# Query products and two gated embeddings of a streaming encoder step, read as pairs of column groups

## The chip, the cores and the metric

The kernel runs on one core of one Trainium2 chip. The metric is the time of one execution on the device, in microseconds (us). Before the change it is 3810.11 us, the median of 3 runs (3791.88 to 3811.25).

## What is computed

One step of a one-layer streaming encoder, in fp32, on 512 prompt frames and 64 running frames of width 2048. The reference, cut to what matters:

```python
a = rmsnorm(x);  z = a @ w_in                       # 2048 x 7168, and 8 gate columns
mix = concat(retention(z), mlstm(z)) @ w_out        # 2048 x 2048, chunk by chunk, with states
h = x + mix
c = rmsnorm(h);  q = c @ w_peer_q                   # 2048 x 2048: 8 heads of 256
s1, s2 = q[..., :128] @ keys1.T, q[..., 128:] @ keys2.T
# top 16 of s1 and of s2, top 16 of their sums: 128 experts of 16384 for each frame
h = h + sum_k softmax(score)_k * gelu(c . peer_u[idx_k]) * peer_v[idx_k]
e = rmsnorm(h)
h = h + sigmoid(e @ w_ple_gate) * (p @ w_ple_proj)  # 2048 x 2048 and 256 x 2048
y = rmsnorm(h)
```

## The kernel before, in words

**Tiles.** Frames are handled in five blocks of 128 (`NB`): four of the prompt, and one (`SB`) that holds the 64 running frames twice. The dense part of the layer is done in three chains, `GROUPS = [[0], [1, 2], [3, SB]]`. A chain is the product with `w_in` in 14 column groups of 512 columns, with retention and mLSTM beside it on all engines, the product with `w_out` in 4 groups, and the query product with `w_peer_q` in 4 groups, in which every group also gives the scores of two heads (`pe_scores`, line 1047). Embeddings (`EMBEDS = [[0], [1, 2, 3], [SB]]`) come later, 4 groups each (`pe_embed`, line 1143).

**Weights.** All products read their weights through one buffer `W` of four slots (q = 0 to 3), 1 MB each. SyncE issues one transfer for each slot (`load_w`, line 601) as soon as TensorE has done with the slot's last content: the semaphore `used[q]`, or `mm` for a slot whose last use ends a group. Without pairing a transfer holds 4 k-tiles of 128 rows by 512 columns, and runs in pieces of 2048 bytes (line 618); four transfers make one column group. With `paired(what, g)` (line 83) a transfer holds 2 k-tiles by 1024 columns, in pieces of 4096 bytes (line 614), and eight transfers make two column groups, which both end at the eighth (`pe_pairs`, line 819). Before the change the `in` and `out` products of chains 1 and 2 are paired; chain 0, all query products and all embeddings are not.

**Experts.** Each frame's experts are gathered by rows: gather number u brings, for the 128 frames of a block, one row of 8 KB of `peer_u` each (1 MB in all, `ring`), and VectorE takes its product with the frame (line 2135). GpSimd issues these gathers (line 766), on a queue of its own. For blocks 0, 3 and `SB` a row of `peer_v` is gathered as well, 12 rows later, and VectorE adds it to `h` (line 2147). Blocks 1 and 2 get their `peer_v` part densely: a matrix of weights is built from one-hot products (`dve_build`, `act_build`, `pe_build`: line 1109), kept in DRAM and multiplied with all of `peer_v` (`pe_dense`, line 1139; 32 steps of 4 MB through `W` and a second buffer). The ring has 8 slots of 1 MB: 4 for u and 4 for v rows up to row 128, 6 for u rows from 128 to 383, then 3 and 3. There are 576 u rows and 320 v rows.

**Order.** Every engine but TensorE follows one list, merged before the launch from generators by their positions (`braid`). The position's unit is one u row: `yield x` puts what follows at row x. `CHAIN_AT`, `EMBED_AT`, `FIRST_PICK`, `LATE_PICKS`, `BUILD_AT` and `DENSE_AT` say at which rows a piece of a chain stands, and `in_at`, `out_at`, `q_at`, `pick_at`, `group_at` turn them into positions. An engine takes its list in order, so VectorE can wait at a piece of a chain while rows lie ready in the ring. For chain 1 `q_at(1, x)` is row 102.6 + 4.7x, for chain 2 `q_at(2, x)` is row 310.6 + 8.2x. The first choice of experts of a chain (`dve_picks`, line 1932 on, at `pick_at`) stands at `q_at(g, 1.5)`: rows 109.7 and 322.9, spread over 4 and 10 rows. The build of block 1's matrix waits at row 350 for the end of chain 2's query product (line 2027). The products of embedding e with the sigmoid are taken by VectorE at `group_at(e, i, ...)` (lines 2078 and 2082): for e = 0 rows 139.4, 142.9, 146.5 and 150.0 (i = 0 to 3), for e = 1 rows 544.7, 551.9, 559.2 and 566.4, at each of these three blocks one after the other, 0.3 row apart.

**TensorE.** Its order is written out: chain 0, chain 1, embedding 0, chain 2, build, dense part, embedding 1, embedding 2. In `pe_product` a piece of `p @ w_ple_proj` (`beside`, line 1186, its matmuls in line 1194) follows the products of its block; there is one bank for it in each half of PSUM, so for the second and third block it waits until VectorE has taken the block before (`e_mul`). `room` (line 1180) waits until the sigmoids of the group that used the banks last are done. Embedding 2 starts when all v rows are in (`v_used`, before line 1163). `pe_h_turn` (line 1018) transposes quarters of `h` for the query product, through banks 2 and 6 in turns.

## Time and profile before

| | |
|---|---|
| median of 3 runs | 3810.11 us (3791.88 to 3811.25) |
| the profiled execution | 3817.56 us |
| its span | 3815.7 us |
| TensorE, VectorE, ScalarE, GpSimd busy | 83%, 72%, 18%, 35% of the span |
| mean TensorE clock granted | 0.899 |
| moved by DMA | 1470.90 MB, 385 GB/s over the span |

Durations and start times in the profile are microseconds from the start of the span. A row of a timeline names start, duration, engine, line, operation, operands and, in brackets, the idle time before it and what ended it. A row of a table by stretches gives for each stretch busy time of the engines with instruction counts, then the granted clock of TensorE (1.00 is the higher of its two levels), the DMA engines' busy share and what they moved in GB/s. Queue q0 is that of GpSimd's gathers, q1 that of SyncE's transfers.

### The profile page before, as it was taken

What the parts mean: (1) busy time and instruction counts of PE and PEld (TensorE: products, weight loads), DVE (VectorE), ACT (ScalarE), POOL (GpSimd) and SP (SyncE); (2) the same over time, 40 slices, a digit from 0 to 9 for tenths busy, and PEclk for the clock granted to TensorE, in tenths of its full rate; (3) what the DMA queues carried; (4) which work ended last, traced back from release to release, by engine and by line L of the source; (5) the groups of instructions that cost most, each with busy time, mean ns of one, the idle gap of its engine ahead of it and who ended that gap; (6) DMA issues with size and microseconds to landing.
All of it is one profiled execution on the core that took longest, in us unless ns stands there. A gap on an engine that the chain in (4) does not pass through costs nothing.

```text
span 3815.7 us, 27395 instructions
## 1 busy us (share of the span) xinstructions
PE 3148.9 (83%) x9486; PEld 1696.0 (44%) x9486; DVE 2762.2 (72%) x3853; ACT 679.6 (18%) x1648; POOL 1329.1 (35%) x905
## 2 busy tenths in 40 slices
PE   8998697998885559999888645699999999888927
PEld 4447343544464234454437635344444444343403
DVE  1005987677677778878757788878788999787772
ACT  2212110222020221123202457000000000011003
POOL 0001533224235444423333522433333333246460
PEclk9999798999997769999998756899999999998968
DMA  7889999999999999999899999999999999999995
GB/s 268 283 274 342 418 417 418 417 418 419 416 398 414 390 362 417 417 417 397 328 402 408 377 365 337 357 420 420 420 420 420 420 419 412 411 417 397 413 370 185
DMA packets 333059, 1470.90 MB, mean 385 GB/s; under 512 B 28152, under 2 KB 66488, under 8 KB 198712
## 3 DMA queue, kind: packets, MB, share of 16 engines
q0 software_dynamic: 129744, 944.82, 60.6%
q1 hardware_dynamic: 192528, 512.40, 35.3%
q10 hardware_dynamic: 10648, 11.92, 1.0%
q8 instruction: 75, 1.23, 0.1%
q14 instruction: 64, 0.52, 0.0%
HBM read 1443.36 MB, written 25.69 MB: 385 GB/s over the span
## 4 chain that ended last, share of the span: by engine, by line
DMA 41%; PE 24%; DVE 9%; issue 5%; POOL 5%; ACT 3%; SPq 0%; DVEq 0%; ACTq 0%; POOLq 0%
DMA ring<-in_peer_v,eidx 21%; PE psum L830 13%; DMA ring<-in_peer_u,eidx 9%; POOL ring L766 5%; DMA W<-in_w_peer_q 5%; PE psum L808 4%; DVE ring L2135 3%; DVE arena L2147 3%; PE psum L1076 2%; PE psum L1139 2%; DMA a_scratch<-arena 1%; DMA W<-in_w_out 1%; DMA W<-in_w_ple_gate 1%; PE psum L1109 1%; PE psum L1194 1%
## 5 line engine op out<-in xcount | busy, mean ns | idle before, releaser
L766 POOL DMA_INDIRECT ring<-in_peer_u,eidx x576 | 879.6, 1527 | 1739.4 <-DVE dots L2135 1310.1
L2135 DVE CUSTOM_DVE_ANT_0 ring<-ring,cx 128x2048 f32<-128x2048 f32 x576 | 1312.1, 2285 | 207.5 <-DMA ring<-in_peer_u,eidx 205.5
L2147 DVE SCALAR_TENSOR_TENSOR arena<-ring,wts,arena 128x2048 f32<-128x2048 f32 x320 | 751.8, 2349 | 210.7 <-DMA ring<-in_peer_v,eidx 194.4
L830 PE MATMUL psum<-W,actT 128*128 128x512 f32 x1792 | 785.9, 597 | 14.0 <-DVE arena L1891 10.6
L766 POOL DMA_INDIRECT ring<-in_peer_v,eidx x320 | 446.3, 1395 | 632.6 <-DVE arena L2147 595.1
L830 PEld LDWEIGHTS psum<-W,actT 128*128 128x128 f32 x1792 | 339.7, 192 | 428.2 <-issue 417.2
L1139 PE MATMUL psum<-arena 128*128 128x512 f32 x1024 | 455.2, 605 | 22.1 <-DVE arena L2058 22.1
L808 PE MATMUL psum<-W,actT 128*128 128x512 f32 x960 | 432.3, 607 | 40.1 <-issue 28.0
L1139 PE MATMUL psum<-W,arena 128*128 128x512 f32 x1024 | 447.2, 596 | 8.7 <-DVE arena L2058 8.7
L1076 PE MATMUL psum<-actT,W 128*128 128x128 f32 (+2 forms) x1536 | 289.9, 354 | 82.8 <-DMA W<-in_w_peer_q 71.4
L1139 PEld LDWEIGHTS psum<-arena 128*128 128x128 f32 x1024 | 197.6, 195 | 269.6 <-issue 239.4
L1076 PEld LDWEIGHTS psum<-actT,W 128*128 128x128 f32 x1536 | 265.1, 210 | 106.6 <-DMA W<-in_w_peer_q 77.0
L808 PEld LDWEIGHTS psum<-W,actT 128*128 128x128 f32 x960 | 185.8, 195 | 272.7 <-issue 256.5
L1139 PEld LDWEIGHTS psum<-W,arena 128*128 128x128 f32 x1024 | 193.8, 191 | 251.1 <-issue 235.7
L830 PE MATMUL psum<-W,arena 128*128 128x512 f32 x512 | 228.5, 608 | 22.5 <-DMA W<-in_w_out 22.2
L1628 ACT ACTIVATE gel<-dots 128x8 f32<-128x8 f32 x72 | 15.1, 209 | 1098.4 <-DVE dots L2135 1098.3
L2058 DVE TENSOR_TENSOR arena<-psum,arena 128x1024 f32<-128x1024 f32 x128 | 155.8, 1218 | 29.3 <-PE psum L1139 29.3
L830 PEld LDWEIGHTS psum<-W,arena 128*128 128x128 f32 x512 | 99.3, 196 | 147.6 <-issue 121.0
L1550 ACT COPY arena<-psum 128x1024 f32<-128x1024 f32 x32 | 32.3, 1009 | 486.5 <-PE psum L1123 486.5
L808 PE MATMUL psum<-W,arena 128*128 128x512 f32 x256 | 113.7, 594 | 0.3 <-ACT arena L1431 0.3
L1109 PE MATMUL psum<-W 128*128 128x128 f32 x256 | 61.9, 422 | 44.3 <-ACT W L1525 24.2
L781 ACT ACTIVATE actT<-psum,gT 128x128 f32<-128x128 f32 x224 | 60.4, 409 | 182.6 <-PE psum L773 108.1
(283 smaller groups left out, 2149.1 us busy)
## 6 DMA issues: line engine op xcount, KB each, us to landing
W<-in_w_in SPq DMA_DIRECT2D x168, 1024.0 KB, 12.8
W<-in_peer_v SPq DMA_DIRECT2D x64, 1024.0 KB, 14.9
arena<-in_peer_v SPq DMA_DIRECT2D x64, 1024.0 KB, 17.6
W<-in_w_out SPq DMA_DIRECT2D x48, 1024.0 KB, 13.0
W<-in_w_peer_q SPq DMA_DIRECT2D x48, 1024.0 KB, 23.0
W<-in_w_ple_gate SPq DMA_DIRECT2D x48, 1024.0 KB, 16.3
actT<-a_scratch SPq DMA_DIRECT2D x64, 256.0 KB, 26.7
ring<-in_peer_u,eidx POOLq DMA_INDIRECT x576, 16.3
```

The source lines that it names most:

```text
L766: pool.indirect_dma_start(ring[:, slot, :], None, a["peer_u" if what == "u" else "peer_v"][0], off(ix, 0)).then_inc(ring_in[slot], 16)
L781: ins = act.activation(aT(k, j), bank(src_bank)[:, x * P:(x + 1) * P], ACT.Identity, scale=gT[:, gain, k:k + 1])
L808: ins = pe.matmul(bank(4 * s + j), lhs(k, j), W[:, k, :], start=(k == 0), stop=(k == KT - 1))
L830: ins = pe.matmul(bank(4 * s + j), lhs(at_k, j), w_pair(q)[:, k, s * CG:(s + 1) * CG], start=(at_k == 0), stop=(at_k == KT - 1))
L1076: ins = pe.matmul(bank(2 * (i % 2) + c // 2)[:, at:at + fresh], W[:, k, c * P:(c + 1) * P], actT[:, k, 0:fresh], start=(k == 0 and c % 2 = ...
L1109: ins = pe.matmul(bank(b % 4)[:, x * P:(x + 1) * P], hot1(b)[:, x, :], hot2(b)[:, x, :], start=True, stop=True)
L1139: ins = pe.matmul(bank(at % 3 * 2 + half), a_turned(m)[:, i // 2, x, :], v_tiles(m)[:, x, c0:c0 + 512], start=(x == 0), stop=(x == VT - 1))
L1194: ins = pe.matmul(bank(4 * (i % 2) + 3), pT(e)[:, k, at:at + P], wp[:, k, i * CG:(i + 1) * CG], start=(k == 0), stop=(k == PK - 1))
L1550: act.copy(a_turned(m).rearrange("p b x t -> p b (x t)"), psum[:, 6:8, :]).then_inc(at_c, 1)
L2058: dve.tensor_tensor(hc, psum[:, at % 3 * 2:at % 3 * 2 + 2, :], hc, ALU.add).then_inc(d_add, 1)
L2135: dve.tensor_tensor_reduce(row, row, cx[:, :], 1.0, 0.0, ALU.mult, ALU.add, dots[:, n % DEEP, c:c + 1]).then_inc(u_used, 1)
L2147: dve.scalar_tensor_tensor(out=hslot(t), in0=ring[:, slot, :], scalar=wts[:, n % DEEP, c:c + 1], in1=hslot(t), op0=ALU.mult, op1=ALU.add). ...
```

## The change

`paired` becomes true for the query products of chains 1 and 2 and for embeddings 0 and 1. `pe_pairs` takes over the pieces beside the products of an embedding: `beside(i, 0)` before the last step, all others of both groups after it. `pe_scores` gets a form for pairs: products of both groups in banks 0 to 3, the scores of the first group before the next pair's first step, those of the second after it. Quarter 2 of `h` is turned through bank 6 and quarter 3 through bank 4. ScalarE takes both groups' queries and then both groups' scores. The first choice of experts moves from `q_at(g, 1.5)` to `q_at(g, 2.6)`: rows 114.8 and 331.9. `group_at` moves to rows 142.9, 143.9, 150.0 and 151.0 for embedding 0, and to rows 551.9, 554.9, 566.4 and 569.4 for embedding 1.

```diff
 def paired(what, g):
 
-    return g > 0 and what in ("in", "out")
+    return g < 2 if what == "ple" else g > 0
...
     if i == j == 0:
-        return q_at(g, 1.5) + FIRST_PICK[g] * x
+        return q_at(g, 2.6) + FIRST_PICK[g] * x
...
 def group_at(e, i, x):
 
-    return embed_at(e, 4 + 2.2 * len(EMBEDS[e]) * (i + 1)) + x
+    n = len(EMBEDS[e])
+    if paired("ple", e):
+        return embed_at(e, 4 + 2.2 * n * (2 * (i // 2) + 2)) + n * (i % 2) + x
+    return embed_at(e, 4 + 2.2 * n * (i + 1)) + x
...
         def pe_pairs(pe, what, g, n, lhs, room, at, side, beside=None):
             for i in range(0, ZG if what == "in" else DG, 2):
                 for step in range(2 * WQ):
                     U, q = prod.use0[what, g] + i + step // WQ, step % WQ
                     pe.wait_ge(landed[q], 16 * (U + 1))
                     for s in range(2):
+                        if beside and step == 2 * WQ - 1 and s == 0:
+                            beside(i, 0)
                         for j in range(n):
...
+                    if beside and step == 2 * WQ - 1:
+                        for s in range(2):
+                            for j in range(0 if s else 1, n):
+                                beside(i + s, j)
...
+        def h_bank(g, q):
+
+            return (2, 6, 6, 4)[q] if g else (2, 6)[q % 2]
+
...
+            if paired("q", g):
+                for i in range(0, DG, 2):
+                    for step in range(2 * WQ):
+                        U, q = prod.use0["q", g] + i + step // WQ, step % WQ
+                        pe.wait_ge(landed[q], 16 * (U + 1))
+                        if i == 0 and step % 2 == 0:
+                            pe.wait_ge(n_cp, counts.quarter0["ffn", g] + (step // 2 + 1) * n)
+                        if i == step == 0:
+                            pe.wait_ge(added, DG * b0 + 3 * n)
+                        if i and step == 0:
+                            score(i - 2)
+                        for s in range(2):
+                            for c in range(4):
+                                if i and step == 0 and c % 2 == 0:
+                                    pe.wait_ge(q_taken, HH * g + 4 * (i - 2 + s) + c + 2)
+                                for k in range(2):
+                                    at_k, at = 2 * step + k, c % 2 * MAXB * P
+                                    ins = pe.matmul(bank(2 * s + c // 2)[:, at:at + fresh],
+                                                    w_pair(q)[:, k, s * CG + c * P:s * CG + (c + 1) * P], actT[:, at_k, 0:fresh],
+                                                    start=(at_k == 0 and c % 2 == 0), stop=(at_k == KT - 1 and c % 2 == 1))
+                                if step == 2 * WQ - 1:
+                                    ins.then_inc(mm, 1)
+                        if step < 2 * WQ - 1:
+                            ins.then_inc(used[q], 1)
+                        if i == 0 and step < 2:
+                            pe_h_turn(pe, g, DG - 2 + step)
+                        if i and step == 0:
+                            score(i - 1)
+                score(DG - 2)
+                score(DG - 1)
+                return
...
-                for i in range(DG):
+                def take_q(i):
                     done = HH * g + 4 * i
-                    yield q_at(g, i + 1)
+                    yield q_at(g, done_at(g, i))
...
+                together = 2 if g else 1
+                for i in range(0, DG, together):
+                    for x in range(together):
+                        yield from take_q(i + x)
+                    for x in range(together):
+                        yield from take_scores(i + x)
```

## Rows read from the trace of the kernel before

**Rows 1.** The page: span, and GB/s in 40 equal slices of it.
```profile
span 3815.7 us, 27395 instructions
GB/s 268 283 274 342 418 417 418 417 418 419 416 398 414 390 362 417 417 417 397 328 402 408 377 365 337 357 420 420 420 420 420 420 419 412 411 417 397 413 370 185
```

**Rows 2.** DMA view, 622 to 640 us: queue, packets, MB, share (pieces of 4 KB against rows).
```profile
q0 software_dynamic: 670, 4.90, 65.5%
q1 hardware_dynamic: 667, 2.60, 36.1%
```

**Rows 3.** DMA view, 2104 to 2140 us (pieces of 2 KB against rows).
```profile
q0 software_dynamic: 1652, 12.00, 80.7%
q1 hardware_dynamic: 1460, 2.89, 21.3%
```

**Rows 4.** DMA view, 650 to 840 us (4 KB), then 3600 to 3680 us (2 KB).
```profile
q1 hardware_dynamic: 5712, 22.02, 28.9%
...
q1 hardware_dynamic: 2661, 5.26, 17.5%
```

**Rows 5.** Busy time by stretches of 20 us (columns as told above).
```profile
1120.00:1140.00 20.00, 17.75 (x74) 14.84 (x73) 15.91 (x17) 3.18 (x8) 8.78 (x5) 0.83 0.91 350
1320.00:1340.00 20.00, 19.26 (x41) 8.46 (x42) 8.02 (x8) 3.46 (x4) 5.59 (x3) 0.91 0.78 283
2140.00:2160.00 20.00, 12.79 (x71) 12.09 (x70) 8.96 (x13) 5.45 (x23) 6.05 (x3) 0.90 0.74 307
2160.00:2180.00 20.00, 12.46 (x55) 11.31 (x56) 20.00 (x40) 19.37 (x47) 6.32 (x7) 0.61 0.95 353
```

**Rows 6.** VectorE's timeline: waits for query products and for embedding 0.
```profile
1093.13 0.29 DVE L1922 MAX8 arena<-arena 128x8 f32<-128x128 f32 x1 [6.78 <-ACT arena L1495]
1328.61 0.69 DVE L2078 TENSOR_TENSOR arena<-psum,arena 128x512 f32<-128x512 f32 x1 [21.31 <-ACT arena L1591]
1344.07 0.69 DVE L2078 TENSOR_TENSOR arena<-psum,arena 128x512 f32<-128x512 f32 x1 [7.40 <-ACT arena L1591]
1360.16 0.69 DVE L2078 TENSOR_TENSOR arena<-psum,arena 128x512 f32<-128x512 f32 x1 [2.61 <-ACT arena L1591]
2154.67 0.23 DVE L2027 TENSOR_SCALAR W<-eidx 128x128 uint32<-128x128 uint32 x1 [10.83 <-PE psum L1076]
```

**Rows 7.** TensorE's timeline: four of 16 query steps that waited for weights.
```profile
1071.10 8.86 PE L1076 MATMUL psum<-actT,W 128*128 128x256 f32 x32 [3.25 <-DMA W<-in_w_peer_q]
1118.73 8.86 PE L1076 MATMUL psum<-actT,W 128*128 128x256 f32 x32 [3.46 <-DMA W<-in_w_peer_q]
2135.78 7.76 PE L1076 MATMUL psum<-actT,W 128*128 128x192 f32 x32 [6.25 <-DMA W<-in_w_peer_q]
2147.69 6.94 PE L1076 MATMUL psum<-actT,W 128*128 128x192 f32 x32 [4.15 <-DMA W<-in_w_peer_q]
```

**Rows 8.** VectorE's timeline: two u rows in a row with a v row between.
```profile
1178.07 2.29 DVE L2135 CUSTOM_DVE_ANT_0 ring<-ring,cx 128x2048 f32<-128x2048 f32 x1 [0.87 <-DMA ring<-in_peer_u,eidx]
1184.49 2.29 DVE L2135 CUSTOM_DVE_ANT_0 ring<-ring,cx 128x2048 f32<-128x2048 f32 x1 [0.89 <-DMA ring<-in_peer_u,eidx]
```

**Rows 9.** TensorE's timeline: embedding 1, then the start of embedding 2.
```profile
3445.75 9.80 PE L808 MATMUL psum<-W,actT 128*128 128x512 f32 x16 [17.77 <-issue]
3458.83 7.03 PE L808 MATMUL psum<-W,actT 128*128 128x512 f32 x16
3469.13 7.03 PE L808 MATMUL psum<-W,actT 128*128 128x512 f32 x16
3642.92 1.88 PE L1194 MATMUL psum<-arena,ring 128*128 128x512 f32 x4
3728.78 6.51 PE L1163 MATMUL psum<-arena,misc 128*128 128x512 f32 x8 [83.98 <-DVE arena L2147]
```

**Rows 10.** VectorE's timeline: embedding 1 at rows 551.9, 566.4, 567.0; a late v row.
```profile
3543.00 0.69 DVE L2078 TENSOR_TENSOR arena<-psum,arena 128x512 f32<-128x512 f32 x1
3636.93 0.69 DVE L2078 TENSOR_TENSOR arena<-psum,arena 128x512 f32<-128x512 f32 x1
3645.66 0.69 DVE L2078 TENSOR_TENSOR arena<-psum,arena 128x512 f32<-128x512 f32 x1 [2.28 <-ACT arena L1591]
3695.33 2.35 DVE L2147 SCALAR_TENSOR_TENSOR arena<-ring,wts,arena 128x2048 f32<-128x2048 f32 x1 [2.56 <-DMA ring<-in_peer_v,eidx]
```

More of the change, by code:

```diff
@@ L795, in pe_product @@
             if paired(what, g):
-                pe_pairs(pe, what, g, n, lhs, room, at, side)
+                pe_pairs(pe, what, g, n, lhs, room, at, side, beside)
                 return side
@@ L817, in pe_product, with pe_pairs @@
             return side
-        def pe_pairs(pe, what, g, n, lhs, room, at, side):
+        def pe_pairs(pe, what, g, n, lhs, room, at, side, beside=None):
             for i in range(0, ZG if what == "in" else DG, 2):
@@ L1021, in pe_h_turn @@
                 pe.wait_ge(added, DG * b0 + q * n + j + 1)
-                if q >= 2:
-                    pe.wait_ge(n_cp, counts.quarter0["ffn", g] + (q - 2) * n + j + 1)
-                pe_turn(pe, "ffn", g, q, j, n, hslot(t), (2, 6)[q % 2] + j)
+                if q >= 2 and not (g and q == 3):
+                    pe.wait_ge(n_cp, counts.quarter0["ffn", g] + (q - (1 if g else 2)) * n + j + 1)
+                pe_turn(pe, "ffn", g, q, j, n, hslot(t), h_bank(g, q) + j)
         def pe_out(pe, g):
@@ L1081, in pe_scores @@
                         ins.then_inc(used[q], 1)
-                    if i == 0 and q == 0 and g:
-                        pe_h_turn(pe, g, DG - 2)
                     if i == 0 and q == 1:
@@ L1455, in turned @@
                 for j in range(n):
[L1456 removed]
+                    act_turned(act, "ffn", g, q, j, n, 1, h_bank(g, q) + j)
             def exps():
@@ L1486, in scores, with take_scores @@
                         act.copy(qT[:, c, 0:fresh], src).then_inc(q_taken, 1)
-                    yield q_at(g, i + 1.4)
+                def take_scores(i):
+                    done = HH * g + 4 * i
+                    yield q_at(g, done_at(g, i) + (0.3 if g else 0.4))
                     if i == 0:
```

4 lines of the change are left out of this document (2 added, 2 removed).

## The prediction

> **What bounds the kernel now.** I read the bytes by slices first [rows 1]. From 400 us to nearly the end they stand near 417 GB/s, a level that no slice passes by more than 3: for most of the span the DMA engines are full, and the time is the bytes divided by that level, plus the stretches where they are not full. So a change here gains in two ways only: cheaper bytes, or fewer stretches with idle DMA. The stretches that this change touches are in the table of 20 us [rows 5]: 350 GB/s at 1120 us (query product of chain 1), 283 at 1320 (embedding 0), 307 and 353 at 2140 (end of chain 2's query product). Against 418 GB/s that is 68, 135, 111 and 65 GB/s missing for 20 us each: 3.3, 6.5, 5.3 and 3.1 us of lost transfer time.
>
> VectorE's timeline says why [rows 6]. Its list is fixed, so when it waits at a piece of a chain, rows pile up in the ring, the ring fills, and then the gathers stop. It waited 6.78 us for chain 1's first scores, 31.3 us in all at embedding 0 (21.31, 7.40, 2.61), and 10.83 us at row 350 for the last step of chain 2's query product. All of these wait for TensorE, and TensorE waits for weights: 16 query steps did so [rows 7]. Those steps come 11.9 us apart (2135.78 to 2147.69), where one needs 7 to 9 us.
>
> Why the weights are slow is the step on which I rest most. SyncE's and GpSimd's queues compete. With pieces of 2 KB, 1460 of them went beside 1652 pieces of the row queue (8 KB rows and some small ones) in 36 us [rows 3]: nearly one for one, so weights got 2.89 MB against 12.00, or 80 GB/s, 13.1 us for a transfer of 1.049 MB. With pieces of 4 KB it was 667 beside 670 in 18 us [rows 2], again one for one, but 2.60 MB against 4.90: 144 GB/s, 7.3 us a transfer. The change makes query and embedding pieces 4 KB, so against a full ring their transfers should come in 7.3 us, not 13.1, and rows should be slower while they do.
>
> **The change part by part.**
>
> *Cheaper bytes.* 16 transfers each for two query products and two embeddings, 64 in all. Time per byte while a piece is in an engine: 22.02 MB in 28.9% of 190 us is 401 GB/s for 4 KB, 5.26 MB in 17.5% of 80 us is 376 for 2 KB [rows 4]. A transfer costs 2.61 instead of 2.79 us of all engines, 0.18 us less. Over 64 that is 11.5 us at most, none if DMA isn't the limit. Embedding 1's 16 fall where I expect another limit (below), so I take 48: -8.6 us; ends -11.5 and 0. The Trainium skill, Perfetto Trace Analysis, section DMA Optimizations, says that going from 2 KB to 4 KB or 8 KB can improve throughput dramatically. By the rows it is 7%, and only on these bytes; the page gives no figure, so the sum goes by the rows.
>
> *Chain 1's query product.* Both groups now end at the eighth transfer, which before was TensorE's step at 1118.73 [rows 7], 48 us after the fourth at 1071.10. The choice of experts stands 5.2 rows later in VectorE's list. A row, u and v, takes 6.42 us when DMA is full [rows 8]: 33 us. With the old transfers VectorE would wait 15 us longer. At 7.3 us a transfer the four steps more are 29 us, and the transfer before them comes sooner too, so the wait of 6.78 us goes. What is late next is nothing: the first row of block 1 is 13 rows off. I return the lost transfer time: -3 us; ends -6.8 and +15 (48 less 33, if transfers stay slow).
>
> *Chain 2's query product.* The choice moves 9 rows, from 322.9 to 331.9, still before row 350. The product ends after 12 transfers at 7.3 us, near 2110 instead of 2154, so the wait of 10.83 us goes. But row 350 can't be reached before its bytes: weights that came in after VectorE's arrival now come before it, and the ring is no longer filled for free. So I take the lost transfer time of the two stretches, 8.4 us: -8; ends -10.8 and 0. The build behind it is a chain on VectorE, ScalarE and TensorE and just starts earlier. h's third and fourth quarters are turned through other banks (16 transposes, as before): nothing, they lie beside weights in flight.
>
> *Embedding 0.* VectorE now asks for nothing at row 139.4, for two groups at 143 and two at 150. The first pair needs eight transfers, four of them there beforehand: four times 7.3 us from about 1278 gives 1312, and results near 1316, against 1328 for the second group before. The wait of 31.3 us falls to about 20. Again DMA limits what is returned, to the 6.5 us lost there: -5; ends 0 and -20. Chain 2 starts that much sooner.
>
> *Embedding 1.* Here the change costs. TensorE issues all pieces beside the products of both groups after step 8, and the one of the second group's third block waits until VectorE has taken its second, at row 555.3. Behind that wait stands everything on TensorE, the second pair's products first. Before, group 2 waited for row 545 only. Steps are 10.3 us [rows 9]; pair 0 ends at 3445.75 + 82 = 3528. VectorE was at row 551.9 at 3543.00 and at 566.4 at 3636.93 [rows 10], 6.5 us a row, so it passes 555.6 near 3567. From there 8 steps, 82 us, the pieces, and some 3 us for the half clock after the gap (the step at 3445.75, after 17.77 us idle, took 9.80 where 7.03 is the rule [rows 9]) give 3656 for the last block of group 2. VectorE stands at it from 3637 on; before it was through at 3646. Then three products of group 3, 5 us with their waits, are still to come. VectorE's remaining rows don't catch up: the last v rows run at the pace of three slots (waits of 2.56 us and the like [rows 10]), and embedding 2 starts when they are in [rows 9]. 3656 - 3646 + 5, less 2 for rows that were ready in the ring: +13 us; ends 0 (if rows fetched in the gap make up for it) and +25.
>
> **Sum.** -8.6 - 3 - 8 - 5 + 13 = -11.6 us against the profiled execution's 3817.56, that is 3806. That execution is 7.5 us above the median of the three runs, so for the median: 3798.
>
> **The rivals.**
>
> *A. The waits come back whole.* If VectorE and the build, not DMA, set the pace around those waits, -6.8 - 10.8 - 20 stand in place of -3 - 8 - 5, with -11.5 for the bytes: -36 with the tail's +13, 3774. For it: VectorE is busy all 20 us of the stretch behind row 350 [rows 5]. Against it: DMA is full almost everywhere [rows 1].
>
> *B. Only the bytes get cheaper.* What is returned is taken again in the next stretch, because the chains end in waits of their own: -8.6 + 13 = +4, 3814. No measurable change.
>
> *C. Slower: results come as pairs, and weights no faster.* If the share of the weights stayed at 80 GB/s, the eighth transfer of chain 1 would keep its time, VectorE would wait 15 us more there and, by the same count, some 12 us at row 331.9 of chain 2 (eight transfers against nine rows), the waits at row 350 and in embedding 0 would stay, and the tail costs 13: 15 + 12 + 13 - 9 = +31, 3841. It decides from about 8 us a transfer: the 33 us that the choice stands later, over the four steps more that it needs. The counts of pieces speak against it [rows 2, 3]. The Trainium skill, DMA: Bandwidth & Descriptors, section SWDGE vs HWDGE vs iDMA, calls a packet of preferably at most 4096 bytes the unit at which an engine changes queues. By that rule larger pieces would bring a queue no larger share, and C would hold; the counts [rows 2, 3] contradict it.
>
> **How the numbers follow.** Forecast 0.48, A 0.25, B 0.17, C 0.07, the rest something else. About 0.5%, 19 us, is what a measurement of this kernel can tell from no change: faster means under 3791, slower over 3829. All of A and a quarter of the forecast's own spread (3785 to 3812) are faster, 0.37; C and a tail at +25 are slower, 0.08; the rest, 0.55, is the same. The range reaches from A, 3773, to 3822 (B with a worse tail).
>
> **What would show it.** Weights against rows in the query products at about 1 to 2 in bytes; query steps that wait for weights 7 to 8 us apart, not 11.9 [rows 7]; no VectorE wait at row 350 and none over 5 us at the first choice; waits at embedding 0 near 20 us; bytes of those stretches near 417 GB/s. In the tail, a gap on TensorE of 30 to 40 us in the middle of embedding 1, ended by VectorE, and a VectorE wait of 10 to 20 us at row 566.4. I am wrong if the share stays at 1 to 4, if the gap in the tail is there and v rows still end as early relative to the dense part, or if a new wait stands at rows 114.8 or 331.9.

## The result, and the profile after

The changed kernel takes **3840.07 us** (median of 19 runs, 3821.12 to 3847.31) against 3810.11: ratio **1.0076** [1.0063, 1.0089], 29 us slower. The forecast was 3798, and its range ended at 3822. Some time near this was among the rivals (C, 3841), but by a mechanism that the trace rules out, as will be seen. The profiled execution has a span of 3845.5 us. Ratios leave out executions in a slower state, of which there was one: ask_tight once took 5259.70 us, its five others 3829 to 3845.

The page of the changed kernel, span and GB/s in 40 slices [rows 1]:

```profile
span 3845.5 us, 27383 instructions
GB/s 267 283 275 342 418 417 418 418 418 419 417 417 399 418 313 418 417 417 399 292 417 417 392 354 339 377 419 420 420 420 420 420 418 411 412 397 419 374 282 191
```

Against [rows 1], slices 12 and 14 have risen from 398 and 390 to 417 and 418, but slice 13 between them has fallen from 414 to 399 and slice 15 (1346 to 1442 us, behind embedding 0) from 362 to 313. In the tail slices 38 and 39 have fallen from 413 and 370 to 374 and 282. What is gained about the queries is lost right behind, and the tail has lost more.

**The weights did come faster.** DMA view of the changed kernel, 1100 to 1140 us, then 2060 to 2110 us, both within a query product (queue, packets, MB, share) [rows 3]:

```profile
q0 software_dynamic: 1554, 11.31, 68.2%
q1 hardware_dynamic: 1386, 5.35, 33.3%
...
q0 software_dynamic: 1867, 13.60, 65.5%
q1 hardware_dynamic: 1867, 7.22, 36.0%
```

1867 pieces went beside 1867, and the bytes are 7.22 against 13.60 MB, about 1 to 2, where they had been 1 to 4 in [rows 3]. In 50 us the weights got 144 GB/s, the 7.3 us a transfer of the forecast. With this larger share rival C falls. The Trainium skill, DMA: Bandwidth & Descriptors, section SWDGE vs HWDGE vs iDMA, names a packet of preferably at most 4096 bytes as the unit at which an engine changes queues. Read so, larger pieces would have brought no larger share. The counts of this stretch and of [rows 3] speak against that reading; those of the run in2_single, further below, do not.

TensorE's timeline of the changed kernel, chain 1's query product, then embedding 0 [rows 7]:

```profile
1062.97 41.60 PE L1094 MATMUL psum<-actT,W 128*128 128x256 f32 x192
...
1289.27 3.70 PE L835 MATMUL psum<-W,actT 128*128 128x512 f32 x8 [2.01 <-DMA W<-in_w_ple_gate]
1296.49 6.51 PE L835 MATMUL psum<-W,actT 128*128 128x512 f32 x8 [3.52 <-DMA W<-in_w_ple_gate]
1303.91 3.70 PE L835 MATMUL psum<-W,actT 128*128 128x512 f32 x8 [0.91 <-DMA W<-in_w_ple_gate]
```

Six query steps of 32 matmuls ran in 41.60 us without a wait, 6.9 us each; the steps of embedding 0 come 7.2 and 7.4 us apart. VectorE no longer waits at the first choices of experts nor at row 350: the 6.78 and 10.83 us [rows 6] are gone.

**Embedding 0 became a longer wait.** VectorE's timeline of the changed kernel [rows 6]:

```profile
1317.44 0.69 DVE L2130 TENSOR_TENSOR arena<-psum,arena 128x512 f32<-128x512 f32 x1 [13.76 <-ACT arena L1643]
1364.97 0.69 DVE L2130 TENSOR_TENSOR arena<-psum,arena 128x512 f32<-128x512 f32 x1 [26.09 <-ACT arena L1643]
```

Together 39.9 us, against 31.3 for the three waits before. The second is long enough to fill the ring and then to leave the DMA engines without work, as the stretches of the changed kernel show (columns as [rows 5]); the third row is the one behind the start of the build:

```profile
1340.00:1360.00 20.00, 14.62 (x23) 5.62 (x22) 0.00 (x0) 0.00 (x0) 0.09 (x1) 0.76 1.00 406
1360.00:1380.00 20.00, 8.73 (x22) 3.78 (x20) 14.68 (x37) 6.35 (x8) 5.08 (x3) 0.76 0.66 229
...
2180.00:2200.00 20.00, 10.17 (x40) 8.90 (x40) 11.85 (x27) 13.71 (x37) 3.59 (x4) 0.50 0.94 332
```

From 1340 to 1360 VectorE does nothing at all; right behind it 229 GB/s are moved where 417 could be, 9 us of lost transfer.

**The tail.** TensorE's timeline of the changed kernel: pieces of `p @ w_ple_proj` after pair 0, first step of pair 1, pieces of group 3, start of embedding 2 [rows 9]:

```profile
3550.87 3.78 PE L1237 MATMUL psum<-arena,ring 128*128 128x512 f32 x4 [19.42 <-DVE arena L2130]
3571.58 3.78 PE L1237 MATMUL psum<-arena,ring 128*128 128x512 f32 x4 [12.37 <-DVE arena L2130]
3578.03 3.60 PE L835 MATMUL psum<-W,actT 128*128 128x512 f32 x8
...
3683.32 3.78 PE L1237 MATMUL psum<-arena,ring 128*128 128x512 f32 x4 [14.74 <-DVE arena L2130]
...
3759.73 5.39 PE L1206 MATMUL psum<-arena,misc 128*128 128x512 f32 x8 [68.04 <-DVE arena L2199]
```

VectorE's timeline of the changed kernel, the asking side of the same [rows 10]:

```profile
3550.13 0.69 DVE L2130 TENSOR_TENSOR arena<-psum,arena 128x512 f32<-128x512 f32 x1
3554.76 0.69 DVE L2130 TENSOR_TENSOR arena<-psum,arena 128x512 f32<-128x512 f32 x1 [3.22 <-PE psum L1237]
...
3654.49 0.69 DVE L2130 TENSOR_TENSOR arena<-psum,arena 128x512 f32<-128x512 f32 x1 [10.37 <-ACT arena L1643]
3664.14 0.69 DVE L2130 TENSOR_TENSOR arena<-psum,arena 128x512 f32<-128x512 f32 x1 [8.23 <-PE psum L1237]
3670.03 0.69 DVE L2130 TENSOR_TENSOR arena<-psum,arena 128x512 f32<-128x512 f32 x1 [2.27 <-ACT arena L1643]
...
3687.21 0.69 DVE L2130 TENSOR_TENSOR arena<-psum,arena 128x512 f32<-128x512 f32 x1 [3.22 <-PE psum L1237]
```

Pair 0 is done on TensorE at 3531.4 (the last step's row at 3529.57 and its 1.88 us). From there to 3578.03, 47 us, TensorE does nothing but these pieces, 13 us of work. So pair 1 ends late, VectorE waits 10.37, 8.23 and 2.27 us for it, and in that time the ring of three and three slots fills. Stretches of 20 us of the changed kernel, then of the kernel before:

```profile
3640.00:3660.00 20.00, 20.00 (x47) 8.77 (x47) 4.54 (x5) 2.66 (x3) 1.87 (x2) 1.00 1.02 409
3660.00:3680.00 20.00, 7.73 (x18) 2.96 (x16) 13.52 (x11) 3.44 (x5) 6.34 (x4) 0.78 0.47 162
3680.00:3700.00 20.00, 7.52 (x8) 2.35 (x8) 15.72 (x16) 1.97 (x2) 9.08 (x6) 0.59 0.73 281
```

```profile
3640.00:3660.00 20.00, 4.80 (x12) 1.82 (x10) 17.66 (x14) 3.46 (x4) 10.10 (x6) 0.73 1.02 415
3660.00:3680.00 20.00, 0.00 (x0) 0.00 (x0) 19.06 (x14) 0.00 (x0) 16.16 (x8) 0.50 1.01 422
3680.00:3700.00 20.00, 0.00 (x0) 0.00 (x0) 16.07 (x10) 0.21 (x1) 11.14 (x6) 0.50 0.83 313
```

To weigh this in all kernels alike, I took from VectorE's timelines the start of u rows 528, 558 and 570, and from TensorE's the start of embedding 2. Stages in us, one profiled execution each; the labels are those of the experiments below. Of the sum, "blocks" is the time that VectorE waited before the products of embedding 1, and "rows" what it waited for gathers into the ring. The last two columns are the ratio to the kernel before and its 95% interval:

| kernel | row 528 to 558 | 558 to 570 | 570 to embedding 2 | sum | blocks | rows | ratio to before | interval |
|---|---|---|---|---|---|---|---|---|
| before | 190.9 | 79.2 | 70.6 | 340.7 | 16.8 | 42.5 | 1 | |
| the change | 199.7 | 99.0 | 71.2 | 369.8 | 31.5 | 54.3 | 1.0076 | 1.0063 to 1.0089 |
| no_ple1 | 191.0 | 78.7 | 71.0 | 340.6 | 17.3 | 42.2 | 1.0005 | 0.9976 to 1.0034 |
| asked_as_made (same kernel) | 191.8 | 78.7 | 70.9 | 341.3 | 17.6 | 42.7 | 0.9983 | 0.9965 to 1.0000 |
| ple1_alone | 200.9 | 99.8 | 70.7 | 371.4 | 31.9 | 56.6 | 1.0075 | 1.0045 to 1.0105 |
| ask_early | 195.2 | 84.4 | 67.9 | 347.4 | 10.9 | 53.4 | 1.0037 | 1.0014 to 1.0059 |
| ask_earlier | 217.0 | 86.1 | 70.7 | 373.8 | 36.4 | 54.7 | 1.0077 | 1.0062 to 1.0093 |
| ask_late | 201.0 | 76.4 | 85.0 | 362.4 | 15.6 | 61.1 | 1.0074 | 1.0045 to 1.0103 |
| ask_both | 198.1 | 78.4 | 83.7 | 360.3 | 14.0 | 62.2 | 1.0076 | 1.0051 to 1.0100 |
| ask_tight | 199.8 | 87.0 | 62.9 | 349.7 | 13.3 | 52.5 | 1.0065 | 1.0044 to 1.0087 |

The sum of the change is 29.1 us over that of before, the whole of what the medians differ. It has two parts of like size: VectorE waits 14.7 us more for the blocks, and 11.8 us more for rows; 2.5 us are other waits. The first part goes and comes with the places at which VectorE asks; the second, 10 us or more, stands in every kernel of this table with embedding 1 in pairs.

Ahead of row 528 the two traces differ by 1.9 us (3388.0 and 3389.9). But there one execution says little: kernels that are alike up to embedding 1 (before, ple1_alone, ask_early, ask_late, ask_both, ask_tight, ask_earlier) reach row 528 between 3366.3 and 3402.8 us. In the tail, the nine traces with embedding 1 in single groups lie within 3 us of one another, from 338.5 to 341.4. So sums of the tail are read from traces. Up to row 200, behind embedding 0, traces repeat as well: these same seven, alike up to there, start it between 1547.4 and 1549.9 us. What lies between, from row 200 to row 528, is left to the medians of many runs.

### The profile page after: what moved, and what is told of

It reads as the page before. It is cut to its first block, busy times and chain, and to the rows that moved or that the text cites. A ratio compares the mean times of both kernels' runs of the same rounds, so it can differ in the third digit from the quotient of the medians.

```text
span 3845.5 us, 27383 instructions
## 1 busy us (share of the span) xinstructions
PE 3141.6 (82%) x9486; PEld 1678.5 (44%) x9486; DVE 2763.9 (72%) x3853; ACT 676.4 (18%) x1646; POOL 1300.3 (34%) x905
## 4 chain that ended last, share of the span: by engine, by line
DMA 43%; PE 20%; DVE 12%; issue 6%; ACT 3%; POOL 3%; SPq 0%; DVEq 0%; ACTq 0%; POOLq 0%
DMA ring<-in_peer_v,eidx 25%; PE psum L835 13%; DMA ring<-in_peer_u,eidx 11%; DVE ring L2187 4%; DVE arena L2199 4%; POOL ring L769 3%; PE psum L1182 2%; DMA W<-in_w_ple_gate 2%; PE psum L811 1%; DMA a_scratch<-arena 1%; DMA a_scratch<-W 1%; DMA arena<-in_state_mlstm_C 1%; PE psum L1237 1%; PE psum L1152 1%; DMA W<-in_w_out 1%
## 5 line engine op out<-in xcount | busy, mean ns | idle before, releaser
L769 POOL DMA_INDIRECT ring<-in_peer_u,eidx x576 | 838.1, 1455 | 1783.9 <-DVE dots L2187 1360.1
L769 POOL DMA_INDIRECT ring<-in_peer_v,eidx x320 | 459.0, 1434 | 648.1 <-DVE arena L2199 609.0
L1182 PE MATMUL psum<-W,arena 128*128 128x512 f32 x1024 | 454.3, 603 | 13.5 <-DVE arena L2110 13.3
L1182 PEld LDWEIGHTS psum<-W,arena 128*128 128x128 f32 x1024 | 195.7, 194 | 261.2 <-issue 236.2
L835 PE MATMUL psum<-W,arena 128*128 128x512 f32 x640 | 288.1, 603 | 23.5 <-DMA W<-in_w_out 23.2
L1094 PE MATMUL psum<-actT,W 128*128 128x256 f32 (+1 forms) x1024 | 202.6, 359 | 33.0 <-DMA W<-in_w_peer_q 19.6
L1094 PEld LDWEIGHTS psum<-actT,W 128*128 128x128 f32 x1024 | 182.9, 193 | 51.9 <-DMA W<-in_w_peer_q 24.3
L835 PEld LDWEIGHTS psum<-W,arena 128*128 128x128 f32 x640 | 122.4, 193 | 179.8 <-issue 147.4
L2130 DVE TENSOR_TENSOR arena<-psum,arena 128x512 f32<-128x512 f32 x20 | 13.8, 688 | 111.9 <-ACT arena L1643 93.0
## 6 DMA issues: line engine op xcount, KB each, us to landing
arena<-in_peer_v SPq DMA_DIRECT2D x64, 1024.0 KB, 17.6
W<-in_w_out SPq DMA_DIRECT2D x48, 1024.0 KB, 17.3
```

What stands on the lines that cost most here:

```text
L769: pool.indirect_dma_start(ring[:, slot, :], None, a["peer_u" if what == "u" else "peer_v"][0], off(ix, 0)).then_inc(ring_in[slot], 16)
L835: ins = pe.matmul(bank(4 * s + j), lhs(at_k, j), w_pair(q)[:, k, s * CG:(s + 1) * CG], start=(at_k == 0), stop=(at_k == KT - 1))
L1094: ins = pe.matmul(bank(2 * s + c // 2)[:, at:at + fresh], w_pair(q)[:, k, s * CG + c * P:s * CG + (c + 1) * P], actT[:, at_k, 0:fresh], st ...
L1182: ins = pe.matmul(bank(at % 3 * 2 + half), a_turned(m)[:, i // 2, x, :], v_tiles(m)[:, x, c0:c0 + 512], start=(x == 0), stop=(x == VT - 1))
```

## The experiments

Fifteen runs were made, of thirteen kernels (asked_as_made is no_ple1 again, asked_later is best again), three or four together on one chip each time. Every ratio is against runs of the kernel before taken beside them; its median went from 3805 to 3818 us between those sittings, so times are compared by ratio and not across them. The ratio on record is not exactly the quotient of the two medians: for most kernels the two lie within 0.1% of each other, but for ask_both they are 1.0076 and 1.0058, for in2_single 1.0107 and 1.0085. Theories are named in the expectations.

### Which part costs

**no_ple1**: the change without embedding 1 in pairs.

```diff
-    return g < 2 if what == "ple" else g > 0
+    return g < 1 if what == "ple" else g > 0
```

> The changed kernel with embedding 1 left unpaired. Theory T (the loss is the order of work in embedding 1): the changed kernel's trace stands only 1.8 us behind before at row 528 and 30 us behind at row 570, so this gives back about 28 us: 3812, ratio 1.000 to 1.001, no TensorE gap of 47 us in embedding 1. Rival U (the loss is made upstream and only shows in the tail, where rows are short of DMA): at most 10 us come back, ratio 1.005 or more.

Measured: 3804.75 beside 3805.24, ratio 1.0005 [0.9976, 1.0034]. The loss is gone, as theory T had it, and what was to be gained is not there either.

**q_only**: query products alone in pairs.

```diff
-    return g < 2 if what == "ple" else g > 0
+    return what != "ple" and g > 0
```

> Only the query products of chains 1 and 2 are paired. Theory T with its upstream part (embedding 0 costs 5 to 6 us on TensorE's chain, which chain 2 carries on; the query products give 3 us back): about 3805, ratio 0.998 to 0.999. My prediction's own terms for the query products (-3 and -8 and -6 for cheaper bytes) would give 3793, ratio 0.9955. Rival (query products cost, for the later first scores): above 1.000.

Measured: 3805.53, ratio 0.9997 [0.9975, 1.0020]. Two waits of VectorE less and 32 cheaper transfers, and nothing of it can be told from no change. The 0.9955 that the prediction's own terms gave lies outside the interval: at most some 10 us of those 17 came back.

**ple1_alone**: the kernel before, and of the change only embedding 1 in pairs, at the changed positions.

```diff
-    return g > 0 and what in ("in", "out")
+    return g == 1 if what == "ple" else g > 0 and what in ("in", "out")
```

> The kernel before with embedding 1 alone paired. Theory T: all of the loss, +28 us, ratio 1.0073. Rival U: under +10, ratio under 1.003. My prediction's term was +13: 1.0034.

Measured: 3835.5, ratio 1.0075 [1.0045, 1.0105], as the whole change. With the first run this shows it from both sides: the loss is embedding 1's.

**ple0_alone**: the same with embedding 0 (`g == 0`).

> The kernel before with embedding 0 alone paired. Theory T: its second pair's eight transfers come at 7.3 us each whatever VectorE does, so it ends some 5 to 8 us later than before, chain 2 carries that on: +4 to +7 us, ratio 1.001 to 1.002. My prediction's term was -5 and -3 for bytes: 0.998. Rival (no effect, DMA makes up): 1.000.

Measured: 3811.72, ratio 1.0021 [0.9998, 1.0045]. No gain; rather a small loss, as theory T had it (1.001 to 1.002), though the interval reaches 1. Its waits are 14.64 and 22.84 us, 37.5 in sum, so the 39.9 of the change do not come from the query products before it. The traces show the loss where it arises: the four with embedding 0 as in the change (the change, no_ple1, ple0_alone, asked_as_made) start row 200 between 1551.2 and 1554.5 us, q_only and the seven alike up to there between 1547.2 and 1549.9. That is some 4 us.

### What in the tail costs: five ways of asking

These are ple1_alone with the positions of VectorE's products shifted. The line is that of `group_at`, which ends in `+ n * (i % 2) + x`; the first pair is i < 2.

```diff
+... - (3 if i < 2 else 0)                ask_early
+... + (0 if i < 2 else 4)                ask_late
+... + (-3 if i < 2 else 4)               ask_both
```

> Embedding 1 alone paired, with VectorE asked for the first pair's blocks 3 rows sooner (rows 548.9 and 551.9). Theory T1 (the time is set by TensorE's gap between the pairs, which VectorE's positions end): the gap of 47 us shrinks by some 20 us, VectorE's waits at row 566.4 (21 us in all) go, and the time is 20 us under that of embedding 1 alone paired: 3815, ratio 1.002. Rival T2 (the gap does not matter, the loss is in the pair as such, both groups' blocks coming at its end): ratio stays at 1.0075.

Measured: 3818.15, ratio 1.0037 [1.0014, 1.0059]: half of the loss is back by the ratio, and more by the tail's sum (371.4 in ple1_alone, 347.4 here). T1 had 1.002 and T2 1.0075, and neither is met. TensorE's timeline of ask_early, the same places as above:

```profile
3526.38 3.70 PE L1204 MATMUL psum<-arena,ring 128*128 128x512 f32 x8 [0.85 <-DVE arena L2088]
3542.45 3.59 PE L1204 MATMUL psum<-arena,ring 128*128 128x512 f32 x4 [12.37 <-DVE arena L2088]
...
3548.72 3.60 PE L835 MATMUL psum<-W,actT 128*128 128x512 f32 x8
```

The wait of 19.42 us is gone, and pair 1 starts at 3548.72 instead of 3578.03. In the second pair VectorE's waits are 2.28 and 2.80 us. The stage of rows 558 to 570 falls by 14.6 us and that before it by 4.5 (against the change). VectorE now waits less for blocks than in the kernel before (10.9 us, 16.8), yet 10.9 us more for rows: that is what is left of the loss in the tail.

> Embedding 1 alone paired, VectorE asked for the second pair's blocks 4 rows later (rows 570.4 and 573.4). TensorE's gap stays at 47 us. Theory T1 in its full form (the payer is VectorE's wait at row 566.4, not TensorE as such, since embedding 2 waits for VectorE's v rows): the waits of 10.4 + 8.2 + 2.3 us mostly go, the time falls by 15 to 20 us: ratio 1.003. Rival T3 (TensorE's lateness is itself on the path): ratio stays at 1.0075.

Measured: 3829.02, ratio 1.0074 [1.0045, 1.0103]: no gain, where T1 in its full form had 1.003. The number is T3's; its mechanism is not shown. VectorE's waits of 21 us are gone, and rows 558 to 570 take 76.4 us, less than in the kernel before. But 14 us come back behind row 570. Stretches of ask_late:

```profile
3660.00:3680.00 20.00, 9.56 (x12) 3.40 (x12) 15.64 (x17) 2.06 (x3) 7.98 (x5) 0.67 0.94 374
3680.00:3700.00 20.00, 5.76 (x8) 1.85 (x8) 16.57 (x14) 2.18 (x3) 5.71 (x4) 0.67 0.49 191
```

The six blocks of the last pair now stand where few u rows are left beside the v rows, and the DMA engines run dry at 3680 us instead of 3660.

> Both shifts together. T1: no wait of VectorE in the second pair, what is left are the ping-pong waits of 3 us between the pieces and VectorE: within 5 us of before, ratio 1.000 to 1.002. T2 or T3: above 1.004.

Measured: 3826.87, ratio 1.0076 [1.0051, 1.0100]. T1 had 1.000 to 1.002, so it fails here. The earlier first pair didn't help where the second was asked late: TensorE was done early and stood 26.79 us for VectorE at 3648.34. The two shifts are not a sum.

**ask_tight**: ask_early, with the second group's blocks 1 row behind the first's and not 3.

```diff
-    ... + n * (i % 2) + x
+    ... + i % 2 + x - (3 if i < 2 else 0)
```

> Embedding 1 alone in pairs, the first pair asked for 3 rows earlier as in the run ask_early, and in each pair the second group's three blocks 1 row behind the first's and not 3. TensorE's pieces beside the products alternate with VectorE, so the order of rows between them costs TensorE time. Theory T1 (what is left of the loss, +7 us in the trace of ask_early, ratio 1.0037, is TensorE standing still between the pairs): the gap between pairs falls by some 10 us, and the time by 5 to 10: ratio 1.001 to 1.0025. Rival (the rest of the loss is that results come as pairs with nothing but v rows on three slots behind them): time as in ask_early, 1.003 to 1.0045, whatever the gap.

Measured: 3834.04 (median of five), ratio 1.0065 [1.0044, 1.0087]. Both expectations are missed on the slow side. TensorE's timeline of ask_tight, first step of pair 1:

```profile
3561.44 3.60 PE L835 MATMUL psum<-W,actT 128*128 128x512 f32 x8
```

Pair 0 ends at 3544.8, so the gap between the pairs is 16.7 us where ask_early has 26.5. It fell by the 10 us that T1 expected, and nothing came back: the tail of the trace is 349.7 us, 2.3 more than ask_early's. So past ask_early the gap is not what costs. The tail is 9.0 us over before, the ratio stands for 25; the rest lies ahead of row 528, where this trace is the latest of its kind (3402.8), and is not explained. The intervals of ask_tight and ask_early overlap.

**ask_earlier**: 6 rows in place of the 3 of ask_early.

> Embedding 1 alone in pairs, its first pair asked for 6 rows before the position of the change (3 rows in ask_early), at row 545.9, near where the first single group's successor stood before. Theory T1 (the gap on TensorE between the pairs is the loss, and it shrinks by some 6.5 us a row of earlier request until VectorE waits for the first pair): VectorE passes row 546 near 3505 and the pair is ready at 3528, so it waits some 20 us; the ring fills meanwhile; the stages from row 528 to the start of embedding 2 come to 345 to 355 us in sum, no better than with 3 rows (347), ratio 1.002 to 1.005. Rival (what counts is only when the second pair can start): 335 to 342 us, as with single groups, ratio 0.999 to 1.001.

Measured: 3846.82, ratio 1.0077 [1.0062, 1.0093], sum of the tail 373.8. VectorE's timeline of ask_earlier, first pair:

```profile
3512.03 0.69 DVE L2088 TENSOR_TENSOR arena<-psum,arena 128x512 f32<-128x512 f32 x1 [14.32 <-ACT arena L1601]
3521.67 0.69 DVE L2088 TENSOR_TENSOR arena<-psum,arena 128x512 f32<-128x512 f32 x1 [8.23 <-PE psum L1204]
```

Both expectations are missed again (345 to 355 us with 1.002 to 1.005, and 335 to 342). Now VectorE is too early: 14.32 and 8.23 us for the first pair, like the 10.37 and 8.23 that the change had in its second, and the stage up to row 558 is 26 us longer than before. The gap between the pairs is 27.1 us, as in ask_early, and the loss is that of ple1_alone. Early by 0, 3 and 6 rows gave 1.0075, 1.0037 and 1.0077. So the gap on TensorE (T1) costs only as far as it makes VectorE wait for blocks, some half of the loss. The best place lies between two waits, and even there VectorE waits some 11 us more for rows than with single groups. That the paired transfers themselves cause this, by their share of the DMA engines, fits the bytes (below), but no run separates it.

### Embedding 0, and what is left of the gain

**ple0_late**: ple0_alone, its second pair asked for 4 rows later (`+ (0 if i < 2 else 4)`).

> Embedding 0 alone paired, VectorE asked for its second pair 4 rows later. The wait of 26 us at row 150 should fall to about 12 and the rows run ahead. Theory T4 (chain 2's start is what costs, since TensorE ends embedding 0 when its 12 transfers are in, at 7.3 us each): the time stays at ratio 1.002. Rival T5 (what costs is VectorE's wait and the DMA idle after it): it falls to 1.000 or under.

Measured: 3806.2, ratio 1.0007 [0.9983, 1.0031] against 1.0021 without the shift; the intervals overlap, so T4 (1.002) and T5 (1.000 or under) are not told apart by it. The second wait falls from 22.84 to 13.45 us, and row 200 starts at 1547.4 instead of 1554.5 us.

**best**: no_ple1 with that same shift.

```diff
-        return embed_at(e, 4 + 2.2 * n * (2 * (i // 2) + 2)) + n * (i % 2) + x
+        return embed_at(e, 4 + 2.2 * n * (2 * (i // 2) + 2)) + n * (i % 2) + x + (0 if i < 2 else 4)
```

> The version that the runs point to: query products of both chains and embedding 0 in pairs, embedding 1 in single groups as before, and the second pair of embedding 0 asked for 4 rows later. Theory D (a core whose DMA engines are full gets nothing from waits that go, and cheaper bytes can't be seen): as the version without embedding 1 in pairs, which stood at 1.0005 of the time before, so 0.998 to 1.001, 3798 to 3812 us. Rival R (the waits of some 40 us at embedding 0 are what hides the gain of the query products, and asking later sets it free): 8 us or more under before, ratio under 0.998. Both expect VectorE's waits at embedding 0 to fall from 40 us in sum to under 20.

Measured: 3803.07 beside 3813.97, ratio **0.9972** [0.9956, 0.9987]. It is faster than the kernel before, clear of noise, and than the change as made, and lies where rival R had it (under 0.998). The waits at embedding 0 are 13.56 and 15.18 us, 28.7 in sum, not under 20 as both theories said.

To see whether the shift does it, both versions ran once more, on one chip:

> The change without embedding 1 in pairs, once more, this time side by side with the version that asks for embedding 0's second pair 4 rows later. Theory N (the parts that were to gain, -16 us and the bytes, came to nothing): ratio 1.000 to 1.002, and the version beside it no more than 0.1% below. Theory B (the bytes' 0.18 us a transfer is there, 48 transfers give -8.6 us, and nothing else is returned): both near 0.9977. Theory R (the waits at embedding 0 eat the gain, and the later request sets it free): this one 1.000, the one beside it 0.997.

> The version that beat both kernels (query products and embedding 0 in pairs, second pair asked for 4 rows later, embedding 1 in single groups), in the same job as the one without the later request. N: 0.999 to 1.001. B: 0.9965 to 0.9985, and the one beside it the same. R: 0.997, the one beside it 1.000.

Measured, with 3817.8 for the kernel before: asked_as_made 3810.02, ratio 0.9983 [0.9965, 1.0000]; asked_later 3801.46, ratio **0.9952** [0.9935, 0.9970]. Stretch of 1300 to 1400 us, which holds embedding 0, in asked_as_made and asked_later, then in ple0_alone and ple0_late:

```profile
1300.00:1400.00 100.00, 53.84 (x113) 22.72 (x112) 63.09 (x124) 11.67 (x18) 33.24 (x20) 0.79 0.97 371
```

```profile
1300.00:1400.00 100.00, 57.86 (x116) 24.09 (x115) 60.90 (x119) 13.93 (x23) 32.03 (x19) 0.82 0.96 375
```

```profile
1300.00:1400.00 100.00, 52.39 (x108) 21.41 (x107) 61.56 (x121) 10.61 (x14) 32.12 (x19) 0.79 0.96 368
```

```profile
1300.00:1400.00 100.00, 59.67 (x136) 27.32 (x136) 68.38 (x130) 17.47 (x32) 37.97 (x21) 0.83 1.02 406
```

In three of four traces with the shift (ple0_late, best, mended) this stretch moves 400 to 406 GB/s, in the four asked as the change has it 354 to 371, and in the kernel before 377: 35 GB/s more over 100 us are some 8 us of transfers at 417. These three start row 200 at 1545.5 to 1547.4 us, some 7 us ahead of the four without the shift and 2 to 3 ahead of the kernels with single groups. The fourth, asked_later, waited 23.95 us all the same, shows 375, and starts row 200 at 1551.1; one execution of a kernel doesn't stand for all. Theory N (nothing returned) doesn't hold for the version with the shift, whose intervals lie below 1 both times. R has the better of B: 0.31% lie between the two versions side by side, though their intervals still meet (0.9965 and 0.9970), and 0.33% between no_ple1 and best, where they overlap. That the shift gains is likely by this, not certain.

**mended**: the whole change, with both shifts that helped.

```diff
+        move = (-3 if e else 0) if i < 2 else (0 if e else 4)
-        return embed_at(e, 4 + 2.2 * n * (2 * (i // 2) + 2)) + n * (i % 2) + x
+        return embed_at(e, 4 + 2.2 * n * (2 * (i // 2) + 2)) + n * (i % 2) + x + move
```

> The whole change, with embedding 1's first pair asked for 3 rows earlier and embedding 0's second pair 4 rows later. If the parts add up: 1.0037 (embedding 1 with the earlier request) and 1.0000 for all else, so 1.003 to 1.0045, against 1.0076 for the change as made. If the two embeddings shift the same rows, so that the parts don't add up, it is under 1.001 or over 1.006.

Measured: 3816.18 beside 3813.97, ratio 1.0010 [0.9995, 1.0026], below the 1.003 to 1.0045 that was expected. That expectation took 1.0000 for all but embedding 1. With the 0.9972 of best in its place the parts do add up: 1.0037 and 0.9972 make 1.0009. Its tail sum is 351.7, 11 us over before, which what lies ahead gives back. Two position shifts took 0.66% off the change as made, and it still isn't as good as leaving embedding 1 alone.

### What the size of pieces is worth by itself

**in2_single**: the kernel before, with the `in` and `out` products of chain 2 taken out of their pairs: 72 transfers back to 2 KB.

```diff
-    return g > 0 and what in ("in", "out")
+    return g == 1 and what in ("in", "out")
```

> The kernel before, with the in and out products of chain 2 in single groups: 72 transfers go back from pieces of 4 KB to pieces of 2 KB, the opposite of the change on a larger number of bytes. Theory B (bytes in 2 KB pieces cost 0.18 us more a transfer, as in the prediction's first term, wherever DMA is full): 72 x 0.18 = +13 us, ratio 1.0034. Theory D (with the DMA engines full, neither the size of pieces nor the share between the queues moves the time, as long as the chain ends in time for the build): 0.999 to 1.002; weights would come in some 13 us instead of 7 against a full ring, so VectorE waits at pieces of the chain, the ring fills, and the weights then come alone. Rival S (the share itself is time): steps of 13.1 us for 7.3 over 72 transfers put chain 2's end hundreds of us later than row 322.9, VectorE waits there with a full ring and the DMA engines idle: ratio over 1.02.

Measured: 3846.39 beside 3813.97, ratio 1.0107 [1.0083, 1.0131]: 41 us by the ratio, 32 by the two medians, between B and S and outside D. DMA view of 1500 to 1540 us, a full stretch: in2_single, then the kernel before.

```profile
DMA packets 4177, 16.36 MB, mean 409 GB/s; under 512 B 265, under 2 KB 265, under 8 KB 2819
q0 software_dynamic: 1529, 11.12, 67.2%
q1 hardware_dynamic: 2631, 5.23, 35.0%
```

```profile
DMA packets 3001, 16.68 MB, mean 417 GB/s; under 512 B 263, under 2 KB 263, under 8 KB 1668
q0 software_dynamic: 1491, 10.90, 65.6%
q1 hardware_dynamic: 1492, 5.76, 35.9%
```

This gives two readings. The 0.32 MB missing are 0.77 us of 40 at 417 GB/s, over 5.0 transfers of weights: 0.15 us a transfer, near the 0.18 of the first term. So bytes in 2 KB pieces are dearer, and 72 x 0.15 makes 11 of the 41 us, if all 72 cost as much as these five. And 2631 pieces went beside 1529: one for one is not a law of its own. Here the weights got 131 GB/s with small pieces. By the traces the loss lies in chain 2: from row 160 to row 383 this trace takes 889.8 us, the seven that are alike up to embedding 1 take 855.1 to 881.7, and the tail is as before (340.9). Which waits it is made of (VectorE stood 11.56 us at one place at 1539 us) wasn't followed further.

## Why the prediction was wrong, point by point

The forecast was -11.6 us, and +29 came. Of these 41 us, 16 are embedding 1's, forecast at +13 and measured at +29. The other 25 are the four gains, -24.6 us in sum: without embedding 1 in pairs the same change stood at 1.0005 and 0.9983, so +2 and -6 us.

**The bound and the share** came as forecast. The DMA engines are full, the weights' share is about 1 to 2 in bytes, and the steps come near 7 us apart. The waits at row 350 and at the first choices are gone. But the reason given, one piece for one whatever its size, doesn't hold: it was read from one stretch at 2 KB [rows 3], and other stretches at 2 KB show larger shares (last section).

**Cheaper bytes, -8.6 us**: the price stands (0.15 against 0.18 us), the sum can't be seen by itself. q_only has 32 such transfers, some 5 us by it, and its interval is 17 us wide.

**Chains 1 and 2, -3 and -8 us**: the waits went and the time hardly showed it. In the trace of the change row 114 comes 7.3 us earlier than before and row 120, behind the moved choice, 11.9 us later, row 132 1.7 earlier. The build starts at 2150.80 instead of 2154.67 us [rows 6], and then ScalarE waits for its writes to DRAM (up to 6.99 us at 2183), with the stretch from 2180 at 332 GB/s, where it had been 403. The forecast had put it as "The build behind it is a chain on VectorE, ScalarE and TensorE and just starts earlier". The step that failed is that lost transfer time, once not lost, was taken as time returned. A likely reason, not shown, is that the rows of the ring had been fetched during the old wait and now compete with those writes.

**Embedding 0, -5 us**: wrong in sign for the waits. The forecast said 31.3 would fall to about 20; it was 39.9. The first pair was ready near 1316, as it had been worked out. The step that failed is that it stopped there and never asked when the second pair is ready: eight steps of 7.3 us behind the first are 1365 to 1370, while VectorE, through with the first pair, stood at row 150 at 1339. By itself it reads 1.0021.

**Embedding 1, +13 us: the term that made it slower**, with +29 measured. Mechanism and places were in part those forecast (a gap of TensorE ended by VectorE, then a wait of 10 us at row 566.4); the sizes were not, and the longer waits for rows had no term. The failing step is "so it passes 555.6 near 3567 [...] 82 us, the pieces, and some 3 us for the half clock [...] give 3656 for the last block of group 2".
- VectorE started on the pair at 3550.13 instead of 3543.00. From 3440 to 3540 us weights took 8.09 MB instead of 6.74 and rows 31.64 instead of 33.02, at 398 GB/s in both: the larger share that helps the weights goes with fewer rows, for which VectorE, and behind it TensorE, then waits. Of the 7.1 us, 1.9 were there at row 528.
- A block that waits for a piece of `p @ w_ple_proj` costs VectorE 3.22 us, for 3.78 us of four matmuls at the lower clock (1.88 us at the higher), and pair 1 started at 3578.03, 11 us later than forecast.
- At the end the blocks come at 3654.49, 3664.14 and 3670.03, in turns with TensorE. The last of group 2 is taken 24.4 us later than before (3645.66 [rows 10]), not 10: 11.0 of the 14.4 us too little is the late start of pair 1.
- The start of embedding 2 is 31.0 us later than before (3759.73 and 3728.78), so 6.6 us come behind that block, where the forecast had 3 (5 less 2).

That rows fetched in the gap would make up for it, the lower end of the term, did not come: with a ring of three and three slots DMA stands while VectorE waits (162 GB/s from 3660 us).

**The rivals.** A (waits come back whole) and C (weights no faster) are both out: C's number was nearly hit, by luck: the share, its ground, went the other way, and of its terms only the wait at embedding 0 stayed. B had all ahead of the tail right, near nothing, if not by cheaper bytes, and the same wrong tail. A tail of +25 stood at the end of the term's own range, and the kernel needed 29 with nothing gained ahead of it: both together lay outside the range of the whole.

**What stays open**: what of the -25 us is real. The version with the later request stood at 0.9972 and 0.9952 and the one without it at 1.0005 and 0.9983, some 12 us apart, of which row 200 shows some 7 in three traces of four. The rest of it, the longer waits for rows in the tail, and the cause of some 30 us in in2_single weren't settled.

## What to carry to other kernels

Taking results in pairs halves how often an engine in a fixed order is asked and lengthens the wait when it comes too early or too late (here 31.3 us became 39.9): work out when each of the two pairs is ready and when the other engine is there, for the second as for the first. Put pairs only where enough other work lies behind them; at the end of the kernel, with a ring of few slots, a wait is not given back. And where the DMA engines are full, a wait that goes away is worth at most what DMA had lost in it, which is read from GB/s, and even that may not come back: by this count the query products were to give 11 us, and q_only could not be told from no change.

## What was not expected of the hardware

- **Shares of the queues.** With 4 KB pieces beside 8 KB rows 1867 went beside 1867, as in [rows 2, 3]. With 2 KB pieces in chain 2's `in` product it was 2631 beside 1529. And the kernel before itself, with 2 KB pieces in chain 1's query product, has 115 GB/s for the weights in a full stretch (DMA view, 1080 to 1120 us):

```profile
q0 software_dynamic: 1622, 11.81, 71.6%
q1 hardware_dynamic: 2312, 4.58, 30.5%
```

  Counts are one for one in some stretches; the 80 GB/s of [rows 3] are no fixed rate of small pieces. What decides between one and nearly two small pieces for a row is open.
- **Small pieces on a full DMA** cost 2% of the whole rate (409 against 417 GB/s) at a third of the bytes. The Trainium skill, Perfetto Trace Analysis, section DMA Optimizations, says that 2 KB to 4 KB or 8 KB can improve throughput dramatically. The size found here is 0.15 us of about 2.6 for a transfer of 1 MB.
- **The clock after the gap.** TensorE's clock stood at its lower level in the gap between the pairs, and the eight matmuls at 3578.03 took 3.60 us, as those at 3526.13 before it. The 3 us set aside for half clock weren't needed there: the four matmuls at 3576.21, the last piece, already took 1.98 us. Stretches of the changed kernel:

```profile
3540.00:3550.00 10.00, 0.00 (x0) 0.00 (x0) 8.26 (x5) 2.76 (x4) 4.97 (x3) 0.50 1.02 423
...
3580.00:3590.00 10.00, 10.00 (x24) 4.37 (x23) 9.96 (x9) 0.00 (x0) 6.79 (x4) 1.00 0.63 225
```

- **Spread of one kernel.** Traces of kernels with the same instructions up to there differ by up to 37 us at row 528 (3366.3 to 3402.8), 1% of the span, while they agree within 3 us at row 200 (1547.4 to 1549.9), and the stage behind row 528 repeats within 3 us where its kernels are alike.
